# FFN up projections as a 2x2 block product in seven products

## Chip, core and metric

The program runs on one core of one Trainium2 chip. The metric is device time in microseconds (us): the median over repeated executions.

## What is computed

One inference step of a two-layer decoder trunk for 512 prompt tokens and 8 x 4 sample tokens, all 544 handled together. Each layer has a gated FFN, a mixing stage (two head-wise recurrences and an LRU branch, then an output projection) and a second gated FFN:

```python
def _swiglu(xn, w_in, w_out):
    gu = xn @ w_in                        # 1024 -> 2 * 2816
    g, u = gu[..., :D_FF], gu[..., D_FF:]
    return (jax.nn.silu(g) * u) @ w_out   # 2816 -> 1024

x = x + 0.5 * _swiglu(_rmsnorm(x, norm_ffn1), w_ffn1_in, w_ffn1_out)
x = x + merged @ w_out                    # the mixing stage
x = x + 0.5 * _swiglu(_rmsnorm(x, norm_ffn2), w_ffn2_in, w_ffn2_out)
```

So an execution has four FFNs: FFN1 and FFN2 of each of two layers. All data are float32.

## The kernel before

Activations lie transposed: `x` is 128 partitions x 8 k tiles x 544 tokens. A float32 product is made of three TensorE passes over operands split into a high part and a low part (the rest): high by high, low weight by high x, high weight by low x (`three_pass`, its matmuls are L415). The names are `wh`, `wl` for the parts of a weight block and `xh`, `xl` for those of x. TensorE takes 272 tokens per matmul, so each k tile costs three passes times two token halves.

An FFN has 22 up blocks. An up block has 2048 columns of weights (8 k tiles, each with 128 columns for g and 128 for u), and gives two output tiles: g into the PSUM pair `stream_a`, u into `stream_b`, 48 matmuls each. The 22 blocks go in two halves, 12 and 10 (`FF_HALVES`). After each half, eight down tiles (one for each k tile of x) multiply the hidden tiles `hh`, `hl` of that half by the down weights and are added to x.

Weights go through two slots. SyncE loads a block into `stage` (L328) as soon as the slot's low part has been made; ScalarE makes the high part (`split_hi`, L847) as soon as TensorE has left the slot's last block; VectorE makes the low part (`split_lo`, L1156) and so releases TensorE for that block. Between these, in program order on each engine:

- VectorE, per up block: g times the root-mean-square factor `rstd` (L1147, `gs`), u times `rstd` (L1147, `us`), their product with the SiLU (L1203), its high part (L1205) and low part (L1206), then the low part of the weights of two blocks on.
- ScalarE, per up block: SiLU (L904), then the high part of a weight block.
- VectorE, per down tile: x plus half the tile (`residual`, L1176). In the second half of an FFN and in the output projection, ScalarE then makes the high part of the new x with the norm's weight (L851) and its square (L892), VectorE the low part (L1162) and the running sum of squares `acc` (L1171). After the last one TensorE sums `acc` over the partitions (L448), ScalarE takes the root, VectorE its reciprocal (L1187).

The wait that orders TensorE behind the weights is `block_ready`; the wait that orders it behind an emptied PSUM pair is on `tile_free`. Register, semaphore and branch instructions stand in the loops (`Fori`); the last block or tile of a loop is written out behind it.

Of the kernel before, what the change touches and what calls it, by code (L numbers as in the profile page):

```python
# [51 lines left out]
FF_HALVES = [12, 10]  # L52
assert sum(FF_HALVES) * P == FF
W_SLOT = 2048


FFN_BLOCKS = sum(FF_HALVES) + 2 * KT
FFN_TILES = 2 * sum(FF_HALVES) + 2 * KT
# [22 lines left out]
STORES = 2 + HEADS * 3 + HEADS * 2 + 4  # L81

# [8 lines left out]
class Chain:  # L91
# [22 lines left out]
    def link(self, ins):  # L114
        self.n += 1
        ins.then_inc(self.sem, 1)
        self.eng.wait_ge(self.sem, self.n)
# [5 lines left out]
def trunk(nc, x_T, w_up1, w_down1, w_mix, w_gates, w_o, w_up2, w_down2, vec, b_if, w_lr2, w_ra, w_ri, consts, level_masks,  # L123
          m0, c0, n0, s0, h0, conv0, o_y, o_pc, o_pm, o_ps, o_ph, o_pconv,
          o_sc, o_sn, o_sm, o_ss, o_sh, o_sconv, rows_dram):
    with ExitStack() as ctx:
# [8 lines left out]
        xh = sb("xh", [P, KT, N], F32R)  # L135
        xl = sb("xl", [P, KT, N], F32R)
        stage = sb("stage", [P, 2, W_SLOT])
        wh = sb("wh", [P, 2, W_SLOT], F32R)
        wl = sb("wl", [P, 2, W_SLOT], F32R)
# [7 lines left out]
        sq = sb("sq", [P, N])  # L147
        xg = sb("xg", [P, N])
# [27 lines left out]
        hh = sb("hh", [P, FF_HALVES[0], N], F32R, ff)  # L176
        hl = sb("hl", [P, FF_HALVES[0], N], F32R, ff)

        gwh, gwl = (t[:, FF_HALVES[1]:FF_HALVES[0], :].rearrange("p t n -> p (t n)")[:, 0:GATE_W] for t in (hh, hl))
        gs = sb("gs", [P, N], where=ff)  # L180
        us = sb("us", [P, N], where=ff)
        sg = sb("sg", [P, N], where=ff)
        hp = sb("hp", [P, N], where=ff)
        gstage = sb("gstage", [P, GATE_W], where=ff)
        ff.close()

# [28 lines left out]
        mh = sb("mh", [P, KT, N], F32R, lru)  # L215
        ml = sb("ml", [P, KT, N], F32R, lru)
# [11 lines left out]
        scv = sb("scv", [P, KT, SEQS, 3], where=lru)  # L228
        lru.close()
# [5 lines left out]
        pair = [psum("stream_a", [P, 2, 512]), psum("stream_b", [P, 2, 512])]  # L235
        Q = psum("mix", [P, 4, 512])

# [12 lines left out]
        first_low = sem("first_low_parts")  # L250
# [53 lines left out]
        first_sq = [merged[:, m, :] for m in range(KT)]  # L304
# [8 lines left out]
        def banks(p):  # L313
            return p[:, :, 0:HALF]

# [6 lines left out]
        def _(sp):  # L322
# [7 lines left out]
            def ffn(L, first, w_up, w_down, gates=False):  # L330
                n = L * LAYER_BLOCKS + first
                up = down = 0
                for half, tiles in enumerate(FF_HALVES):
                    if gates and half == 1:
                        sp.dma_start(gstage[:], w_gates[L]).then_inc(gate_loaded, 16)
# [8 lines left out]
                    n = n + tiles  # L344
                    up += tiles
                    with sp.Fori(0, KT // 2) as i:
                        for j in range(2):
                            load(i * 2 + (n + j), j, w_down[L, i * 2 + (down + j), :, 0:tiles * P])
                    n = n + KT
                    down += KT  # L350

            sp.wait_ge(init_done, 1)
            for L in range(DEPTH):
                ffn(L, 0, w_up1, w_down1, gates=True)
# [6 lines left out]
                ffn(L, BLK_FFN2, w_up2, w_down2)  # L361
# [10 lines left out]
        def _(pool):  # L372
# [5 lines left out]
            pool.memset(ones[:], 1.0)  # L378
            pool.memset(one_t[:], 1.0).then_inc(split_done, 2)
# [30 lines left out]
        def _(pe):  # L410
# [10 lines left out]
            def tile(t, slot, k_tiles, width, col, act=(xh, xl), weights=(wh, wl), late=None, fresh=None,  # L421
                     count=1, ks=None, low=None):
# [5 lines left out]
                if ks[0] == 0:  # L428
                    pe.wait_ge(tile_free, t + 1)
                for k in ks:  # L430
                    if late and k >= k_tiles - 2:
                        late(k_tiles - 1 - k)
                    if low is not None:
                        pe.wait_ge(low, k + 1)
# [10 lines left out]
            def norm_squares():  # L445

                for h in range(2):
                    mm = pe.matmul(Q[:, h, 0:HALF], ones[:], acc[:, h * HALF:(h + 1) * HALF], start=True, stop=True)  # L448
                return mm

            def first_block(n, t, j, norm):

                parts = (wh[:, j], wl[:, j])
                block_ready(n)
                tile(t, 0, KT, 2 * P, 0, weights=parts, low=first_low)
                tile(t + 1, 1, KT, 2 * P, P, weights=parts, ks=range(KT // 2))
                pe.wait_ge(acc_ready, norm)
                norm_squares().then_inc(norm_sum, 1)
                tile(t + 1, 1, KT, 2 * P, P, weights=parts, ks=range(KT // 2, KT))

            def ffn_in_block(L, n, t, j, norm=None):
                if norm == KT:
                    return first_block(n, t, j, norm)
                block_ready(n)
                tile(t, 0, KT, 2 * P, 0, weights=(wh[:, j], wl[:, j]), fresh=norm)
                if norm is not None:
                    pe.wait_ge(acc_ready, norm)
                    norm_squares().then_inc(norm_sum, 1)
                tile(t + 1, 1, KT, 2 * P, P, weights=(wh[:, j], wl[:, j]))

            def ffn(L, first, first_tile, h_base, norm):
                n = L * LAYER_BLOCKS + first
                t = L * LAYER_TILES + first_tile
                hd = L * (2 * sum(FF_HALVES)) + h_base
                for half, tiles in enumerate(FF_HALVES):
                    start = 0
                    if half == 0:
                        for j in range(2):
                            ffn_in_block(L, n + j, t + 2 * j, j, norm if j == 0 else None)
                        start = 1  # L480
                    with pe.Fori(start, tiles // 2) as i:
                        for j in range(2):
                            ffn_in_block(L, i * 2 + (n + j), i * 4 + (t + 2 * j), j)
# [1425 lines left out]
```

## Time and profile before

| | |
|---|---|
| median of 3 runs | 3124.23 us (3123.17 to 3125.16) |
| profiled execution: span from the first to the last instruction | 3122.4 us |
| what lies around that span, by the median | 1.8 us |
| TensorE matmul busy | 3063.6 us, 98% |
| VectorE busy | 1902.3 us, 61% |
| ScalarE busy | 1039.4 us, 33% |
| granted TensorE clock, mean | 0.995 |

The profile's busy time of TensorE counts pipelined matmuls, so the pace of a stage is read from the times at which its tiles end. The profiled execution has no time of its own on record beside the span; the difference to the median stands in the table. PE is TensorE, PEld its weight load, DVE is VectorE, ACT is ScalarE, SP is SyncE.

### The profile page before, as it was taken

How to read it: one execution, taken by the hardware profiler on the slowest of the kernel's cores; microseconds unless marked ns; L12 is line 12 of the kernel's file. 1: busy time of each engine (PE TensorE's matmuls, PEld its weight loads, DVE VectorE, ACT ScalarE, POOL GpSimd, SP SyncE). 2: the span in 40 equal slices, each digit the busy share in tenths (PEclk: the TensorE clock that was granted, in tenths of full speed). 3: DMA queues.
4: the chain of work that ended last, by engine and by line, in shares of the span. 5: the costliest groups of instructions: out<-in, count | busy, mean ns of one | idle time of the engine just before them, and what ended most of it. 6: DMA issues, size and time to landing. Idle time of an engine off the chain costs nothing.

```text
span 3122.4 us, 60368 instructions
## 1 busy us (share of the span) xinstructions
PE 3063.6 (98%) x25824; PEld 3014.0 (97%) x25824; DVE 1902.3 (61%) x2705; ACT 1039.4 (33%) x992; POOL 12.9 (0%) x36
## 2 busy tenths in 40 slices
PE   7999999999999999999999999999999999999998
PEld 7999999999999999999999999999999999999997
DVE  5434467778788874434454344677878788643344
ACT  3222232334334652212232122333334466321212
POOL 1000000000000000000000000000000000000000
PEclk9999999999999999999999999999999999999999
DMA  3222233233222222222222222233222222222222
GB/s 141 78 95 94 72 112 109 107 110 111 97 86 91 86 83 95 78 98 76 86 95 81 101 89 73 105 111 134 92 98 98 85 97 80 95 81 84 91 79 71
DMA packets 51915, 292.18 MB, mean 94 GB/s; under 512 B 9384, under 2 KB 12264, under 8 KB 23880
## 3 DMA queue, kind: packets, MB, share of 16 engines
q1 hardware_dynamic: 37152, 241.43, 22.4%
q10 hardware_dynamic: 13984, 48.48, 4.1%
q8 instruction: 90, 1.47, 0.2%
q0 software_dynamic: 656, 0.52, 0.1%
q14 instruction: 33, 0.27, 0.0%
HBM read 268.90 MB, written 21.50 MB: 93 GB/s over the span
## 4 chain that ended last, share of the span: by engine, by line
PE 88%; DVE 7%; ACT 2%; issue 1%; DMA 1%; DVEq 0%; ACTq 0%; POOL 0%; POOLq 0%
PE stream_b L415 38%; PE stream_a L415 38%; PE stream_a L502 4%; PE mix L787 1%; DVE wl L1156 1%; PE stream_b L508 1%; PE mix L623 1%; PE mix L563 1%; PE mix L707 1%; PE mix L544 1%; PE mix L626 1%; PE mix L556 0%; DVE rstd L1187 0%; PE mix L734 0%; DMA seven<-rows_scratch 0%
## 5 line engine op out<-in xcount | busy, mean ns | idle before, releaser
L847 ACT ACTIVATE wh<-stage 128x2048 fp32r<-128x2048 f32 (+2 forms) x246 | 435.9, 1772 | 800.0 <-PE stream_b L415 588.1
L1156 DVE TENSOR_TENSOR wl<-stage,wh 128x2048 fp32r<-128x2048 f32 (+2 forms) x248 | 525.8, 2120 | 93.6 <-ACT wh L847 69.2
L415 PE MATMUL stream_a<-xh,wh 128*128 128x272 f32 x2560 | 536.2, 291 | 18.6 <-DVE xl L1162 13.1
L415 PE MATMUL stream_b<-xh,wh 128*128 128x272 f32 x2560 | 541.2, 293 | 0.0
L415 PE MATMUL stream_a<-xl,wh 128*128 128x272 f32 x2560 | 531.1, 289 | 0.0
L415 PE MATMUL stream_b<-xl,wh 128*128 128x272 f32 x2560 | 530.0, 288 | 0.0
L415 PE MATMUL stream_a<-xh,wl 128*128 128x272 f32 x2560 | 529.5, 288 | 0.0
L415 PE MATMUL stream_b<-xh,wl 128*128 128x272 f32 x2560 | 528.3, 288 | 0.0
L415 PEld LDWEIGHTS stream_a<-xh,wh 128*128 128x128 f32 x2560 | 404.2, 189 | 22.4 <-DVE wl L1156 13.1
L415 PEld LDWEIGHTS stream_b<-xh,wh 128*128 128x128 f32 x2560 | 403.6, 188 | 7.3 <-issue 3.3
L415 PEld LDWEIGHTS stream_a<-xh,wl 128*128 128x128 f32 x2560 | 403.7, 189 | 0.0
L415 PEld LDWEIGHTS stream_b<-xh,wl 128*128 128x128 f32 x2560 | 402.7, 189 | 0.0
L415 PEld LDWEIGHTS stream_a<-xl,wh 128*128 128x128 f32 x2560 | 401.4, 189 | 0.0
L415 PEld LDWEIGHTS stream_b<-xl,wh 128*128 128x128 f32 x2560 | 400.2, 189 | 0.0
L1147 DVE TENSOR_TENSOR us<-stream_b,rstd 128x544 f32<-128x544 f32 x88 | 63.8, 725 | 446.4 <-PE stream_b L415 446.1
L904 ACT ACTIVATE sg<-gs 128x544 f32<-128x544 f32 x88 | 58.0, 660 | 401.1 <-DVE gs L1147 401.1
L415 PE MATMUL stream_a<-hh,wh 128*128 128x272 f32 x704 | 146.0, 289 | 0.0
L415 PE MATMUL stream_b<-hh,wh 128*128 128x272 f32 x704 | 146.0, 289 | 0.0
L415 PE MATMUL stream_a<-hh,wl 128*128 128x272 f32 x704 | 145.6, 288 | 0.0
L415 PE MATMUL stream_b<-hh,wl 128*128 128x272 f32 x704 | 145.6, 288 | 0.0
L502 PE MATMUL stream_a<-wh,xl 128*128 128x256 f32 x512 | 144.7, 283 | 0.0
L415 PE MATMUL stream_a<-hl,wh 128*128 128x272 f32 x704 | 144.1, 286 | 0.0
(349 smaller groups left out, 4367.6 us busy)
## 6 DMA issues: line engine op xcount, KB each, us to landing
stage<-in_w_mix SPq DMA_DIRECT2D x88, 1024.0 KB, 4.8
stage<-in_w_up SPq DMA_DIRECT2D x87, 1024.0 KB, 4.8
stage<-in_w_down SPq DMA_DIRECT2D x32, 768.0 KB, 4.2
stage<-in_w_down SPq DMA_DIRECT2D x32, 640.0 KB, 3.9
CS<-in_c ACTq DMA_DIRECT2D x8, 1024.0 KB, 4.7
out_o_sc<-CS ACTq DMA_DIRECT2D x8, 1024.0 KB
CS<-in_s ACTq DMA_DIRECT2D x8, 1024.0 KB, 4.8
out_o_ss<-CS ACTq DMA_DIRECT2D x8, 1024.0 KB
```

The source lines that it names most:

```text
L415: mm = [pe.matmul(out(h), a(h), b(h), start=f, stop=z) for h in range(2)]
L502: mm = pe.matmul(out, a[:, k, tok], b[:, j, k * DV:(k + 1) * DV], start=f, stop=z)
L508: mm = pe.matmul(pair[1][:, 0, 0:DV], both[:, k * 2 * NS:k * 2 * NS + P], b[:, j, k * DV:(k + 1) * DV], start=f, stop=z)
L544: mm = pe.matmul(Q[g * NS:(g + 1) * NS, b_, 0:DV], Qm[:, s_ * NS:(s_ + 1) * NS], CS[:, s_, :], start=s_ < 4, stop=s_ >= 4)
L563: mm = pe.matmul(Q[:, b_ + h, 0:HALF], ones[:], src[:, h * HALF:(h + 1) * HALF], start=True, stop=True)
L623: mm = pe.matmul(Q[:, v, sl], here, wS[:, sl], start=True, stop=c == 0)
L626: mm = pe.matmul(Q[:, v, sl], before, qs[:, sl], start=False, stop=True)
L707: mm = pe.matmul(Q[g * G:(g + 1) * G, 1 + r // 4, o:o + G], lhs[:, k0:k0 + G], rhs[:, k0:k0 + G], start=True, stop=True)
L847: act.activation(wh[:, slot, 0:width], stage[:, slot, 0:width], ACT.Copy).then_inc(hi_done, 1)
L904: act.activation(sg[:], gs[:], ACT.Silu).then_inc(silu_done, 1)
L1147: ins = tt_(halves(dst), banks(pair[slot]), rs2, ALU.mult)
L1156: tt_(wl[:, slot, 0:width], stage[:, slot, 0:width], wh[:, slot, 0:width].bitcast(F32), ALU.subtract).then_inc(split_done, 1)
```

## The change

In an up block the k tiles are taken in pairs (even, odd) and the tokens in halves. That makes g and u of 128 columns a 2x2 by 2x2 block product, and seven products in place of eight give it. Each product is four k-tile pairs times three passes on 272 tokens, 12 matmuls, so a block has 84 matmuls in place of 96. The products need sums and differences of blocks:

- of the weights: four sums `S` per block (VectorE, L1399, L1405, L1406), whose high part ScalarE and whose low part VectorE makes (L955, L1422); three blocks are used as they are (`wx_high`, `wx_low`, L946, L1418). `S` lies in the same memory as `wl`.
- of x: four sums `XT` per pair of k tiles, with high and low parts (`x_side`), made once per FFN where x is updated ahead of it.
- of the products: ScalarE copies the first product into the third bank (`seed`) and keeps the second in `p5s` (`keep_fifth`); VectorE adds `p5s` to the running third bank twice (`sum_fifth`, L1413), into bank 1 and bank 3, on which the fifth to seventh products then go on. TensorE waits for each of these inside the block.

Blocks use the four banks of `stream` and the four of `mix` in turn. The hidden product is left without the second `rstd`, which `residual_scaled` now puts on the down tile (L1488), with the addition to x in an instruction of its own (L1491). The high part of the hidden tile moves to ScalarE; its low part stays on VectorE. The 22 blocks go in four parts (4, 6, 6, 6) with eight down tiles after each.

```diff
-FF_HALVES = [12, 10]
+FF_PARTS = [4, 6, 6, 6]
...
+        S = sb("w_sums", [P, 2, W_SLOT], F32, own)
+        own.close()
         wl = sb("wl", [P, 2, W_SLOT], F32R)
...
         # TensorE
+            def product(B, bank, w, q, x, seeded, base=None, step=0):
+                for kt in range(PAIRS):
...
+                    for a, b, f, z in ((0, 0, True, False), (1, 0, False, False), (0, 1, False, True)):
+                        mm = pe.matmul(B[:, bank, 0:HALF], w[a][:, kt, q, :], x[b][:, kt, :],
+                                       start=f and kt == 0 and not seeded, stop=z and kt == PAIRS - 1,
+                                       skip_group_check=True)
...
+                block_ready(n)
+                pe.wait_ge(tile_free, t + freed)
+                product(B, 0, pure, 2, xp[0], False, base, 1).then_inc(prod_done, 1)
+                product(B, 1, sums, 0, xt[0], False, base, 2).then_inc(prod_done, 1)
...
+                pe.wait_ge(copied, 2 * u + 1)
+                product(B, 2, sums, 2, xt[1], True, base, 3).then_inc(prod_done, 1)
+                product(B, 0, pure, 0, xp[1], True, base, 4).then_inc(prod_done, 1)
+                pe.wait_ge(seeded, 2 * u + 1)
+                product(B, 2, sums, 1, xt[2], True, base, 3).then_inc(prod_done, 1)
+                product(B, 1, sums, 3, xp[2], True, base, 4).then_inc(prod_done, 1)
+                pe.wait_ge(seeded, 2 * u + 2)
+                product(B, 2, pure, 1, xt[3], True, base, 5).then_inc(tile_done, 2)
...
         # ScalarE, per up block
+                            gate(tj)
+                            pure_high(i + (nh + 1), j, tj + 1, 0)
+                            pure_high(i + (nh + 1), j, tj + 1, 1)
+                            seed(uj + 1, 1 - j, tj + 2, 0)
+                            hidden_high(tj, uj, i * 2 + j)
+                            keep_fifth(uj + 1, 1 - j)
+                            sums_high(uj + 2, j, 0)
+                            sums_high(uj + 2, j, 1)
...
         # VectorE
+            def into_up(nh, u, j):
+                begun = weight_sums(nh, j)
+                more_sums(j, begun)
+                up_low(2 * nh + j, u, j, (lambda: sum_fifth(u - 1, 0, 1)) if j else None)
+                if j:
+                    sum_fifth(u - 1, 0, 3)
...
+            def up_block(t, u, a, j, nh, plain):
+                B = sets[j]
+                dve.wait_ge(prod_done, (PRODUCTS - 1) * u + 6)
+                tt_(halves(gs[:]), banks(B[:, 0:2]), rs2, ALU.mult).then_inc(tile_free, 1)
+                if not plain:
+                    begun = weight_sums(nh, j)
+                dve.wait_ge(silu_done, u + 1)
+                tile_ready(t + 1)
...
+                tt_(halves(hp[:]), halves(sg[:]), banks(B[:, 2:4]), ALU.mult).then_inc(tile_free, 1)
...
+                else:
+                    more_sums(j, begun)
+                    up_low(nh * 2 + j, u + 2, j, lambda: sum_fifth(u + 1, 1 - j, 1))
+                    hidden_low(u, a)
+                    sum_fifth(u + 1, 1 - j, 3)
```

How this stands on VectorE, at three places. First the loop over up blocks: `gs` is now called `xg`, and each row is one instruction with the semaphores that it waits for. Before, one block (written-out end of a half):

```order
L1147 TENSOR_TENSOR gs<-stream_a,rstd 128x544 [waits tile_done]
L1147 TENSOR_TENSOR us<-stream_b,rstd 128x544 [waits tile_done,tile_free]
L1203 TENSOR_TENSOR hp<-sg,us 128x544 [waits silu_done,tile_free]
L1205 CAST hh<-hp 128x544 [waits dve_chain]
L1206 TENSOR_TENSOR hl<-hp,hh 128x544 [waits dve_chain]
L1156 TENSOR_TENSOR wl<-stage,wh 128x1536 [waits hi_done,h_done]
```

and of the change, one block whose slot is filled with another up block:

```order
L1526 TENSOR_TENSOR xg<-stream,rstd 128x544 [waits product_done]
L1399 TENSOR_TENSOR w_sums<-stage 128x4x256 [waits block_loaded_0]
L1533 TENSOR_TENSOR hp<-sg,stream 128x544 [waits h_done,product_seeded,tile_done,silu_done]
L1405 TENSOR_TENSOR w_sums<-stage,w_sums 128x4x128 [waits dve_chain]
L1406 TENSOR_TENSOR w_sums<-stage,w_sums 128x4x128 [waits dve_chain]
L1418 TENSOR_TENSOR wx_low<-stage,wx_high 128x1536 [waits pure_high]
L1413 TENSOR_TENSOR mix<-mix,p5s 128x272 [waits product_copied,product_done]
L1422 TENSOR_TENSOR wl<-w_sums,wh 128x2048 [waits hi_done]
L1520 TENSOR_TENSOR hl<-hp,hh 128x544 [waits hh_done]
L1413 TENSOR_TENSOR mix<-mix,p5s 128x272 [waits product_copied,product_done]
```

The four weight sums, two low parts in place of one and the two additions of `p5s` for the block that TensorE works on have come in between; the multiplication of u and the high part of the hidden tile have gone.

Second the end of a run of down tiles, where the slot of the seventh down tile is filled with the first up block of the next part. Before:

```order
L104 REGISTER_ALU
L111 ISA
L1176 SCALAR_TENSOR_TENSOR x<-stream_a,x 128x544 [waits tile_done]
L1156 TENSOR_TENSOR wl<-stage,wh 128x2048 [waits hi_done,tile_free]
L1176 SCALAR_TENSOR_TENSOR x<-stream_b,x 128x544 [waits tile_done]
L1156 TENSOR_TENSOR wl<-stage,wh 128x2048 [waits hi_done,tile_free]
```

and now, of the first of these two slots and the beginning of the second:

```order
L1488 SCALAR_TENSOR_TENSOR sg<-stream,rstd 128x544 [waits tile_done]
L1491 TENSOR_TENSOR x<-x,sg 128x544 [waits tile_free]
L1399 TENSOR_TENSOR w_sums<-stage 128x4x256 [waits block_loaded_0,x_updated]
L1405 TENSOR_TENSOR w_sums<-stage,w_sums 128x4x128 [waits dve_chain]
L1406 TENSOR_TENSOR w_sums<-stage,w_sums 128x4x128 [waits dve_chain]
L1418 TENSOR_TENSOR wx_low<-stage,wx_high 128x1536 [waits pure_high]
L1422 TENSOR_TENSOR wl<-w_sums,wh 128x2048 [waits hi_done]
L1488 SCALAR_TENSOR_TENSOR sg<-stream,rstd 128x544 [waits tile_done]
L1491 TENSOR_TENSOR x<-x,sg 128x544 [waits tile_free]
```

Two instructions between the end of a down tile and the release of the slot have become seven.

Third the output projection ahead of FFN2. There a block of weights gives two tiles, and after each tile x is updated and prepared for the next stage. Before, the second tile of the loop's last block:

```order
L1176 SCALAR_TENSOR_TENSOR x<-stream_b,x 128x544
L1161 REGISTER_ALU [waits tile_free]
L1162 ISA [waits xh_ready]
L1162 SCALAR_TENSOR_TENSOR xl<-x,vectors,xh 128x544
L1171 TENSOR_TENSOR acc<-acc,sq 128x544 [waits sq_ready]
L1155 REGISTER_ALU [waits acc_ready]
L1156 TENSOR_TENSOR wl<-stage,wh 128x2048 [waits hi_done]
```

and now, the second tile of a block and the slot's next up block:

```order
L1496 SCALAR_TENSOR_TENSOR x<-stream,x 128x544 [waits tile_done]
L1446 TENSOR_TENSOR xt<-x_scaled 128x272 [waits xh_ready,tile_free]
L1447 TENSOR_TENSOR xt<-xt,x_scaled 128x272 [waits dve_chain]
L1451 TENSOR_TENSOR xt<-x_scaled,xt 128x272 [waits x_sums]
L1471 TENSOR_TENSOR acc<-acc,sq 128x544 [waits sq_ready]
L1460 TENSOR_TENSOR xt_low<-xt,xt_high 128x544 [waits x_high,x_sums,acc_ready]
L1462 TENSOR_TENSOR xp_low<-x_scaled,xp_high 128x544 [waits x_high]
L1466 TENSOR_TENSOR xt_low<-xt,xt_high 128x272 [waits x_high]
L1399 TENSOR_TENSOR w_sums<-stage 128x4x256 [waits block_loaded_0]
L1405 TENSOR_TENSOR w_sums<-stage,w_sums 128x4x128 [waits dve_chain]
L1406 TENSOR_TENSOR w_sums<-stage,w_sums 128x4x128 [waits dve_chain]
L1418 TENSOR_TENSOR wx_low<-stage,wx_high 128x1536 [waits pure_high]
```

After each first tile of a pair VectorE has one sum and two low parts, after each second one three sums and three low parts, before the weights of the slot; the second slot's `wl` is followed by the reciprocal (L1507) as before.

## Rows read from the trace of the kernel before

**Rows 1.** Page, busy time by engine and chain that ended last
```profile
PE 3063.6 (98%) x25824; PEld 3014.0 (97%) x25824; DVE 1902.3 (61%) x2705; ACT 1039.4 (33%) x992; POOL 12.9 (0%) x36
PE 88%; DVE 7%; ACT 2%; issue 1%; DMA 1%; DVEq 0%; ACTq 0%; POOL 0%; POOLq 0%
```

**Rows 2.** Chain in order of time: start us, us, what
```profile
31.14 0.14 issue
31.27 7.78 PE stream_a L415 x48
...
57.09 6.01 PE stream_a L415 x48
...
505.15 11.40 PE stream_a L502 x96
...
1310.83 9.00 PE stream_a L415 x72
```

**Rows 3.** Chain in order of time, FFN2 of layer 0 into FFN1 of layer 1
```profile
1555.60 7.50 PE stream_b L415 x60
1563.10 6.01 PE stream_a L415 x48
1569.12 0.92 PE mix L448 x4
```

**Rows 4.** VectorE groups by line and shape: count, busy us, mean ns, idle before
```profile
L1156 DVE TENSOR_TENSOR wl<-stage,wh 128x2048 fp32r<-128x2048 f32 x184 | 421.8, 2292 | 71.5 <-ACT wh L847 49.3 <-ACT wh L857 8.5
L1156 DVE TENSOR_TENSOR wl<-stage,wh 128x1536 fp32r<-128x1536 f32 x32 | 56.3, 1758 | 16.0 <-ACT wh L847 15.6
L1343 DVE TENSOR_TENSOR Kws<-K,seqm 128x1024 fp32r<-128x1024 f32 x16 | 19.5, 1221 | 0.3
L1206 DVE TENSOR_TENSOR hl<-hp,hh 128x544 f32 x72 | 52.3, 726 | 8.8
L1444 DVE TENSOR_TENSOR Kw<-mix,seven 128x512 f32<-128x512 f32 x8 | 5.5, 692 | 0.3
L1624 DVE TENSOR_TENSOR lxp<-stream_b,rstd 128x272 f32<-128x272 f32 x8 | 3.5, 440 | 0.2
L1187 DVE RECIPROCAL rstd<-sd 128x544 f32<-128x544 f32 x6 | 21.3, 3554 | 7.2 <-ACT sd L882 5.4 <-DVE Qm L1739 1.8
```

**Rows 5.** ScalarE groups by line and shape, same columns
```profile
L916 ACT ACTIVATE hh<-gstage 128x1024 fp32r<-128x1024 f32 x2 | 2.1, 1044 | 0.0
L892 ACT ACTIVATE sq<-x 128x544 f32 x40 | 25.8, 645 | 35.5 <-DVE x L1176 35.5
L851 ACT ACTIVATE xh<-x,vectors x34 | 25.5, 750 | 162.7 <-DVE x L1176 162.7
L979 ACT ACTIVATE hsq<-mix 128x256 f32<-128x256 f32 x8 | 3.1, 384 | 39.4 <-PE mix L544 39.4
```

**Rows 6.** Timeline of VectorE: start us, us, instruction, idle before
```profile
12.21 2.87 DVE L1162 SCALAR_TENSOR_TENSOR xl<-x,vectors,xh 128x544 fp32r<-128x544 f32 x4
...
59.44 0.73 DVE L1206 TENSOR_TENSOR hl<-hp,hh 128x544 f32 x1
60.28 2.29 DVE L1156 TENSOR_TENSOR wl<-stage,wh 128x2048 fp32r<-128x2048 f32 x1
```

**Rows 7.** Windows, TensorE: stretch, us, busy (count), granted clock, DMA share, GB/s
```profile
27.00:31.00 4.00, 1.51 (x13) 1.00 0.64 247
33.00:34.00 1.00, 1.00 (x7) 0.50 0.00 0
```

**Rows 8.** DMA issues: count, KB each, median us to landing
```profile
stage<-in_w_down SPq DMA_DIRECT2D x32, 640.0 KB, 3.9
wra<-in_w_ra ACTq DMA_DIRECT2D x4, 256.0 KB, 2.7
```

**Rows 9.** Timeline of ScalarE at the start: start us, us, instruction
```profile
7.98 1.91 ACT L857 ACTIVATE wh<-stage 128x2048 fp32r<-128x2048 f32 x1
9.79 2.65 ACT L851 ACTIVATE xh<-x,vectors 128x544 fp32r<-128x544 f32 x4
```

More of the change, by code:

```diff
@@ L328, in load, with ffn @@
                 sp.dma_start(stage[:, slot, 0:width], src).then_inc(block_loaded[slot], 16)
-            def ffn(L, first, w_up, w_down, gates=False):
+            def ffn(L, first, first_tile, w_up, w_down, gates=False, swapped=False):
                 n = L * LAYER_BLOCKS + first
[L332 to L335, printed above, removed]
+                t = L * LAYER_TILES + first_tile
+                up = 0
+                for part, tiles in enumerate(FF_PARTS):
                     begun = 0
@@ L925, in ffn @@
-                    with act.Fori(0, KT // 2 - 1) as i:
-                        down(i, tiles * P)
-                    down(KT // 2 - 1, 0 if last and half == 1 else 2 * D)
-                    t, nh = t + KT, nh + KT // 2
+                    i = KT // 2 - 1
+                    for j in range(2):
+                        arrived(i, j)
+                        if end and next_ffn is None:
+                            if not last:
+                                plain_high(i + (nh + 1), j, i * 2 + (t + j), 2 * D)
+                        else:
+                            into_up(i + (nh + 1), j, i * 2 + (t + j), u + j, t + KT,
+                                    norm + 1 if end else None)
@@ L1191, in ffn, with up @@
+            def ffn(L, first, first_tile, u, norm, g_col, gates=False, next_ffn=None, last=False):
+                nh = L * (LAYER_BLOCKS // 2) + first // 2
                 t = L * LAYER_TILES + first_tile
[L1192 removed]
                 reciprocal_norm(norm)
[L1194 to L1196 removed]
+                for part, tiles in enumerate(FF_PARTS):
+                    def up(i, plain=0):
                         chain.restart()
@@ L1214, in ffn, with down @@
+                    if part == 0 and gates and L == 0:
                         decay_rates()
-                    n, t, hd = n + tiles, t + 2 * tiles, hd + tiles
-                    if gates and half == 1:
+                    t, nh, u = t + 2 * tiles, nh + tiles // 2, u + tiles
+                    end = part == len(FF_PARTS) - 1
+                    if end:
+                        clear_acc()
+                    def down(i, ahead):
+                        chain.restart()
+                        for j in range(2):
+                            swapped = end and next_ffn is not None
+                            m = i * 2 + (1 - j if swapped else j)
+                            n_sq = norm * KT + i * 2 + (KT + j)
+                            residual_scaled(i * 2 + (t + j), j, m, i * 2 + (down_tiles(L, first) + part * KT + j + 1))
+                            if swapped:
+                                x_side(i, j, n_sq, next_ffn)
+                            elif end:
+                                prepare(m, g_col + m, n_sq, not last)
+                            ahead(i, j)
@@ new lines, in plain, with next_stage @@
+                    def plain(i, j):
+                        split_lo(i * 2 + (2 * nh + 2 + j), j, tiles * P)
+                    def next_stage(i, j):
+                        if not end or next_ffn is not None:
+                            into_up(i + (nh + 1), u + j, j)
+                        elif not last:
+                            split_lo(i * 2 + (2 * nh + 2 + j), j, 2 * D)
+                    with dve.Fori(0, KT // 2 - 1) as i:
+                        down(i, plain)
+                    if gates and end:
```

538 lines of the change are left out of this document (383 added, 155 removed).

## Prediction

> **What bounds the kernel now.** I read the page first: TensorE is busy 98% of the span, VectorE 61%, ScalarE 33%, and the chain that ended last lies 88% on TensorE [rows 1]. Then the chain in order of time: an up tile of 48 matmuls takes 6.01 us, a down tile of 72 takes 9.00 [rows 2], so 0.125 us a matmul of 272 columns wherever nothing is waited for. The hand-over from one FFN to the next shows no gap: 1555.60 + 7.50 is 1563.10, and 1563.10 + 6.01 is 1569.12 within rounding [rows 3]. Removed matmuls are therefore worth their full time, as long as VectorE and ScalarE keep up. They do so easily now: a block lasts 12.02 us and VectorE needs about 5.6 of it (three instructions of 0.725, one copy, one low part of 2.29 [rows 4]). So the prediction is made on VectorE's lists.
>
> **What is removed.** 88 up blocks lose 12 matmuls each: 1056 x 0.1253 = **-132.3 us**. The runs of 12 into one bank cost no more: a tile whose matmuls go 24 in a row into one bank has 96 of 256 columns in 11.40 us [rows 2], 0.1188 each, which is the 272-column pace less 16 columns at 2.4 GHz.
>
> **Prices.** Two-operand VectorE work costs 2.29 us for 2048 columns, 1.76 for 1536, 1.22 for 1024, 0.73 for 544, 0.69 for 512, 0.44 for 272 [rows 4]; 768 lies at 0.96, 1088 at 1.29, 2176 at 2.42 on the same line. ScalarE: 1.04 for 1024, 0.65 for a square of 544, 0.75 for a scaled copy of 544, 0.38 for 256 out of PSUM [rows 5], so 0.41 for 272. A gap between two VectorE instructions is 0.12 where loop registers are set on a wait, and -0.07 where four independent ones overlap (4 x 0.785 took 2.87) [rows 6]; I take 0 inside a list and 0.04 where engines hand over. VectorE writing to PSUM has no row: 0.44 as for reading it, at least the same line's fixed part of 0.16, at most twice 0.44.
>
> **Inside an up part.** An up block is 7 products of 1.503, 10.52 us. VectorE's ten instructions make 9.7 us. What closes the loop is one chain: seventh product of a block, first and second of the next (4.51), ScalarE keeps the second product (0.41) and only then, in its order, makes the high parts of the sums (2 x 1.04), VectorE the low part (2.29), the hidden low part (0.73), and the second addition (0.44), for which the next seventh product waits. With hand-overs that is 10.7, so 0.2 a block. Twelve such blocks an FFN, beside those in the starts below: 48 x 0.2 = **+10**. (Gaps of -0.07: 0; of 0.12: 0.8 each, 38.)
>
> **Twelve boundaries from down tiles to up blocks.** The sums for the next part lie in the memory of the low weights that the seventh down tile reads, and stand behind that tile's eviction on VectorE. From its end: eviction 0.73, addition 0.73, sums 1.22 + 0.69 + 0.69, ScalarE's high parts 2.09, low part 2.29, and six hand-overs: 8.7 us until the block may start. TensorE has only the eighth down tile to cover it: 36 matmuls, 4.5 us, after a part of six; 24, 3.0 us, after the part of four. Before, the same wait was one high and one low part under a tile of 7.5 or 9.0 us. So 8 x 4.2 + 4 x 5.7 = 56, and the first block then waits 0.24 for its first addition, since VectorE comes to it 6.25 us after the start and four products take 6.01: **+59**. (Bounds 53 to 77, by the gaps.)
>
> **Output projection into FFN2, twice.** Per first tile of a pair VectorE has 0.73 (x), a wait for ScalarE's square and scaled copy (1.40), 0.44, 0.72 and two of 0.44: 4.2 us; per second tile 0.73, 1.40, three of 0.44, 0.72, two of 0.73, 0.44: 6.1; two tiles and a low part of weights come to about 13 against 12 us of TensorE, which delays the projection by 1.4. From the start of its last block VectorE still has both tiles of the third (10.3), the sums and low parts of the first slot (7.0 with ScalarE), both tiles of the fourth (10.3), then 4.4 and the addition 0.44 before the fifth product: 33.7 with hand-overs, against 12.0 + 0.92 + 6.01 on TensorE. That is 14.8. Behind it the reciprocal (3.55) stands ahead of the next round, so the second block's first addition comes 9.8 us after the first block's last addition, 2.3 after the products that should cover it; 0.5 more in the third. **+38** in all. (30 to 54.)
>
> **FFN2 of layer 0 into FFN1 of layer 1.** The same preparation now hangs on down tiles of 4.5 us: 5.9 and 7.8 us a pair with eviction, addition and a weight part of 0.96, some 14 with hand-overs against 9.0, for three pairs: 15. Then as above from the eighth tile: 4.9 + 7.0 + 6.8 + 4.4 + 0.44 and hand-overs, 24, against 11.4, and 3 for the reciprocal: 16. **+31.** (27 to 42.)
>
> **FFN1 into the mixing stage, twice.** Eviction, addition, high part, low part, sum and weights make 5.0 against 4.5 a tile: 2, and 2.5 until the gates' tile has the last squares: **+9**. (7 to 16.)
>
> **Start.** ScalarE can begin at 7.98 and scales four k tiles in 2.65 [rows 9]; with 1.49, 2.09 and twice 2.65 all of x is scaled at 16.9. From there VectorE has seven of 1.29, two of 2.42, seven of 0.72 and two additions, 20 us plus waits: 38; then the second slot's 7.0: the second block begins at 45. Its first addition stands behind reciprocal and round, 55; it ends at 60, the third at 71. Before, the third block ended at 57.09 [rows 2]. 14, and 4.5 that the first term already counts: **+18**. (14 to 24.) The last eviction adds an instruction: +1.
>
> **The clock.** At 31.27 a tile took 7.78 in place of 6.01 [rows 2], after a stretch in which TensorE worked 1.51 of 4 us; the clock granted was 1.00 before and 0.50 within the tile [rows 7]. That wait was shorter than any of the twelve. So I charge each boundary 1.77 less the 0.24 it hides: **+18** (0 to 21). The Trainium skill says likewise (TensorE: Matmul & The Clock Gate, "HAM oscillation — how this bites in real kernels") that matmul bursts with waits between pay the slow clock burst by burst. The trace agrees at that one tile; read strictly, it applies to the waits inside the four FFN starts too, and the sum would be 3194 in place of 3176.
>
> **Hidden.** The down weights: a slot's load is issued after the low part, 2.4 us behind a tile's end, and has two tiles less that time; 256 KB landed in 2.7 and 640 KB in 3.9 [rows 8], against 3.6 in the part of four and 6.6 in those of six. ScalarE's new high part of the hidden tile takes 0.65 of a 10.7 us round in which it works 5.9. If the loads weren't covered, up to 1 us for each of 24 tiles.
>
> **Sum.** -132.3 + 10 + 59 + 38 + 31 + 9 + 18 + 1 + 18 = +52 on the profiled 3122.4: 3174; with the 1.8 that the median lies above the span, **3176 us**, slower by 1.7%. A difference of 0.2%, 6 us, is about what can be told from none.
>
> **Rivals.**
> - *VectorE's instructions overlap throughout* and the clock stays up: all terms at their lower ends, 0 + 53 + 30 + 27 + 7 + 14 + 1 = 132, which is just the gain: 3124. For it: four independent ones did overlap [rows 6]; against it: most of the new ones wait for another engine or for their predecessor. 0.08.
> - *Faster: the x sums hide.* If VectorE and ScalarE prepare x and the sums under the tiles they follow, as they do now at hand-overs without a gap [rows 3], the terms of projection, FFN change, mixing and start (96) fall away: 3080. It decides as soon as less than half of them is left. Against it: the lists are two to three times the tiles. 0.10.
> - *Every wait inside a block restarts TensorE.* Four waits a block; the tile at 31.27 began 0.14 after its releaser [rows 2], and if each cost that, 88 x 4 x 0.14 = 49 more: 3225. Against it: a tile that found both its waits fulfilled took 6.01 [rows 2]. 0.10.
> - *The clock rule in the starts*: ten more such stretches, two or three a start, of 1.77 each: 3194. For it, the tile at 31.27; against it, TensorE waits for VectorE's list there whatever its clock. 0.15.
> - *The sum as it stands*, give or take the gaps: 0.57.
>
> **Chances and range.** Faster 0.12 (the second rival and a tail of the first), same 0.04, slower 0.84. Range 3130 to 3235: it leaves out the first two rivals below, and above it gaps of 0.12 everywhere (38 + 77 + 54 + 42 + 16 + 24 + 1 + 21 = 273, so 3265).
>
> **What would show it.** In the profile after: 24,768 matmuls and a few; seven-product blocks of 10.5 to 10.8 us; a TensorE wait of 4 to 6 us on `wl` at each of twelve boundaries; waits of TensorE that sum to over 10 us on x parts and additions at each of the four FFN starts (kernel start, two projections, FFN2 into FFN1); half clock behind the boundaries; VectorE busy near all of the FFNs. I am wrong if blocks last over 11 us (the loop's chain), if the boundaries show no wait (the sums begin earlier than I read), or if the starts cost under 10 us each.

## The result, and the profile after

The changed kernel takes 3184.89 us in the median (3184.57 to 3189.59, 4 runs), the kernel before 3123.7 on the same chip: a ratio of 1.0199, with a 95% interval of 1.0185 to 1.0214. It is slower by 61 us. The profiled execution spans 3182.9 us, 60.5 more than before.

The page of the changed kernel, busy time by engine and the chain that ended last, which answers to [rows 1]:

```profile
PE 2996.2 (94%) x24772; PEld 2934.1 (92%) x24772; DVE 2409.8 (76%) x3398; ACT 1316.6 (41%) x1629; POOL 13.3 (0%) x37
...
PE 76%; DVE 14%; ACT 6%; issue 3%; DMA 1%; DVEq 0%; ACTq 0%; POOL 0%; POOLq 0%
```

There are 1052 matmuls fewer, but the chain now lies 20% on VectorE and ScalarE, against 9% before. What TensorE waits for, longest sums first (us in all, times, longest):

```profile
PE stream L518 <- DVE wl L1422: 70.1, 15, 5.7
PE stream L474 <- DVE wl L1378: 26.3, 18, 6.7
PE stream L518 <- DVE xp_low L1437: 17.1, 3, 16.0
PE stream L474 <- DVE sg L1488: 8.1, 2, 4.0
PE mix L518 <- ACT mix L963: 7.0, 4, 1.9
```

The first line is the low part of the weight sums: twelve boundaries between parts (55.7 us) and three of the FFN starts (14.4). One boundary after a part of six, as the chain of the changed kernel in order of time (start us, us, what); the waits here have no counterpart in [rows 3]:

```profile
218.31 0.74 DVE sg L1488
...
219.06 0.74 DVE x L1491
...
219.82 1.24 DVE w_sums L1399
...
221.08 0.70 DVE w_sums L1405
...
221.81 0.70 DVE w_sums L1406
...
223.50 1.05 ACT wh L955
...
224.57 2.30 DVE wl L1422
226.87 0.04 issue
226.92 13.07 PE stream L518 x84
...
282.21 10.55 PE mix L518 x84
```

The seventh down tile ends at 218.28 and the eighth at 222.78; the block starts at 226.92. In between, 8.6 us, stands the list of the prediction, link by link. The first block then takes 13.07 us, the later ones 10.55. The windows of the same stretch (us, busy of PE, PEld, DVE, ACT, POOL, then the granted clock, the DMA share and GB/s), beside [rows 7]:

```profile
222.00:227.00 5.00, 0.86 (x8) 0.64 (x6) 4.60 (x4) 2.52 (x3) 0.00 (x0) 0.82 0.00 0
227.00:232.00 5.00, 5.00 (x22) 5.00 (x23) 4.42 (x6) 1.34 (x2) 0.00 (x0) 0.50 0.58 210
232.00:240.00 8.00, 8.00 (x66) 8.00 (x65) 5.77 (x6) 2.95 (x4) 0.00 (x0) 1.00 0.20 63
```

For five microseconds behind the wait the granted clock is 0.50, which is 1.2 GHz: 22 matmuls where a full clock gives 40.

The terms of the sum against what the two traces show:

| step of the prediction | predicted, us | measured, us | worked out from |
|---|---|---|---|
| removed matmuls | -132 | -132 | 1056 at the pace of [rows 2] |
| rounds inside a part | +10 | +2 | 10.55 a block against 84 x 0.1253 = 10.52, some 72 blocks |
| twelve boundaries | +59 | +56 | waits of 4.14 after eight parts of six and 5.64 after four of four |
| the clock | +18 | +29 | twelve first blocks, 12.4 to 13.5 each, together 155.9, against 12 x 10.55 |
| projection into FFN2, twice | +38 | +29 | last wait of mixing to end of the fourth block: 96.8 and 98.1 against 89.2 and 88.9, plus 6.0 removed from each |
| FFN2 into FFN1 | +31 | +31 | 109.7 from the last block of FFN2 to the fourth of FFN1, against 36.1 + 0.9 + 42.1 |
| FFN1 into mixing, twice | +9 | +18 | last up block to the sum of squares: 52.2 and 52.5 against 67.3 before, less the 24.1 of down matmuls that now lie in earlier parts |
| start | +18 | +19 | fourth block ends at 81.9 against 69.1, plus 6.0 removed |
| end | +1 | 0 | 53.6 from the last up block to the end against 77.2, less 24.0 of down matmuls that now lie in earlier parts |
| not in the sum: constants of the gates | 0 | +9 | first eight down tiles 33.1, those of the other parts of four 24.5 |
| sum | +52 | +61 | span: +60.5 |

The forecast's +59 for the boundaries holds 12 x 0.24 for the first addition, which lies in the first block and so in the measured 29: the waits alone were forecast at 56 and took 56.

### The profile page after: what moved, and what is told of

It is laid out like the page before. It is cut to its first block, busy times and chain, and to the rows that moved or that the text cites. A ratio compares the mean times of both kernels' runs of the same rounds, so it can differ in the third digit from the quotient of the medians.

```text
span 3182.9 us, 61006 instructions
## 1 busy us (share of the span) xinstructions
PE 2996.2 (94%) x24772; PEld 2934.1 (92%) x24772; DVE 2409.8 (76%) x3398; ACT 1316.6 (41%) x1629; POOL 13.3 (0%) x37
## 4 chain that ended last, share of the span: by engine, by line
PE 76%; DVE 14%; ACT 6%; issue 3%; DMA 1%; DVEq 0%; ACTq 0%; POOL 0%; POOLq 0%
PE stream L474 35%; PE stream L518 14%; PE mix L518 14%; PE stream L585 4%; DVE wl L1378 1%; DVE wl L1422 1%; ACT wh L955 1%; DVE sg L1488 1%; PE mix L870 1%; DVE x L1491 1%; PE stream L591 1%; PE mix L706 1%; PE mix L646 1%; ACT wh L934 1%; DVE rstd L1507 1%
## 5 line engine op out<-in xcount | busy, mean ns | idle before, releaser
L474 PE MATMUL stream<-xh,wh 128*128 128x272 f32 x2304 | 492.1, 295 | 2.5 <-DVE val L1681 2.5
L474 PE MATMUL stream<-xl,wh 128*128 128x272 f32 x2304 | 476.8, 288 | 0.0
L474 PE MATMUL stream<-xh,wl 128*128 128x272 f32 x2304 | 475.7, 288 | 0.6 <-issue 0.6
L474 PEld LDWEIGHTS stream<-xh,wh 128*128 128x128 f32 x2304 | 362.9, 188 | 12.9 <-issue 6.9
L1378 DVE TENSOR_TENSOR wl<-stage,wh 128x768 fp32r<-128x768 f32 (+2 forms) x224 | 334.0, 1491 | 48.2 <-ACT wh L934 32.3
L474 PEld LDWEIGHTS stream<-xh,wl 128*128 128x128 f32 x2304 | 361.9, 188 | 0.8 <-issue 0.8
L474 PEld LDWEIGHTS stream<-xl,wh 128*128 128x128 f32 x2304 | 360.2, 189 | 0.0
L474 PE MATMUL stream<-hh,wh 128*128 128x272 f32 x1408 | 295.8, 291 | 26.6 <-DVE wl L1378 26.3
L474 PE MATMUL stream<-hl,wh 128*128 128x272 f32 x1408 | 292.8, 290 | 0.0
L474 PE MATMUL stream<-hh,wl 128*128 128x272 f32 x1408 | 292.4, 289 | 0.0
L1422 DVE TENSOR_TENSOR wl<-w_sums,wh 128x2048 fp32r<-128x2048 f32 x88 | 201.7, 2292 | 28.9 <-ACT wh L955 28.3
L955 ACT ACTIVATE wh<-w_sums 128x1024 fp32r<-128x1024 f32 x176 | 175.9, 1049 | 37.3 <-DVE w_sums L1406 37.3
L1488 DVE SCALAR_TENSOR_TENSOR sg<-stream,rstd 128x544 f32<-128x544 f32 x128 | 92.5, 723 | 122.9 <-PE stream L474 122.5
```

What stands on the lines that cost most here:

```text
L474: mm = [pe.matmul(out(h), a(h), b(h), start=f, stop=z) for h in range(2)]
L955: ins = act.activation(quads(wh, slot, a, b), quads(S, slot, a, b), ACT.Copy)
L1378: tt_(wl[:, slot, 0:width], stage[:, slot, 0:width], wh[:, slot, 0:width].bitcast(F32), ALU.subtract).then_inc(split_done, 1)
L1422: tt_(wl[:, slot, :], S[:, slot, :], wh[:, slot, :].bitcast(F32), ALU.subtract).then_inc(split_done, 1)
L1488: ins = stt(halves(sg[:]), banks(pair[slot]), 0.5, rs2, ALU.mult, ALU.mult)
```

## The experiments

All are timed against the kernel before on the same chip, which took 3122.9 to 3124.1 us beside them; differences are to the 3184.9 of the changed kernel, unless said otherwise.

**The parts alone** (e1_parts). The kernel before, cut into the parts of the changed one; eight products, none of the sums.

```diff
-FF_HALVES = [12, 10]
+FF_HALVES = [4, 6, 6, 6]
```

> The kernel before with parts of 4, 6, 6, 6 in place of 12, 10 and nothing else: eight products, no sums. Theory A (the boundary stall is the list sums, high parts, low part that stands behind the eviction): from a seventh down tile's end only eviction 0.73, ScalarE's high part 2.0 beside it and the low part 2.29 remain, 4.4 us against 4.5 of cover after a part of six and 3.0 after the part of four; so about 0 at eight boundaries, 1.4 and a slow-clock 1.8 at four, the constants of the gates 7 to 9 once, 2 to 6 at hand-overs: 3124 + 15 to 28, 3139 to 3152. Rival B (short parts cost this by themselves): most of the 85 us that the boundaries of the changed kernel show, 3190 to 3210.

Measured: 3159.4 us, ratio 1.0118 (1.0101 to 1.0135), 36.5 more than before. Its chain at the boundary that was shown above:

```profile
206.29 4.50 PE stream_b L417 x36
210.79 0.04 issue
210.84 4.27 PE stream_a L417 x32
```

No wait after a part of six (0.04 us), 2.0 to 2.1 after a part of four. So rival B falls: short parts don't make the stall, the sums do. Theory A was too low by 8 us at its upper end; some of that lies at the two hand-overs into mixing, where TensorE waits 2.6 us for an eviction (1.0 before). Of the 193 us that the changed kernel pays for its 132, about 36 are the parts' and 157, the rest, come with the seven products.

**TensorE kept at work during the wait** (e2_warm). Extra matmuls on x parts into a bank that nothing reads then, ahead of the first block of a part: 42 behind the part of four, 30 behind those of six.

```diff
+                for _ in range(warm):
+                    pe.matmul(Q[:, 3, 0:HALF], XTH[:, 0, 0, 0:P], XTH[:, 0, 0, :], start=True, stop=True)
                 B = sets[j]
...
-                                 stage_no if first_of_all else None, norm if first_of_all else None)
+                                 stage_no if first_of_all else None, norm if first_of_all else None,
+                                 0 if part == 0 or j else 42 if part == 1 else 30)
```

> The changed kernel, with 30 (after a part of six) or 42 (after the part of four) extra matmuls of 272 columns into an unused bank while TensorE waits at each of the twelve boundaries; 3.8 and 5.3 us of the waits of 4.1 and 5.6. Theory A (the clock falls because TensorE stands still there): the first block of a part goes from 13.0 back to 10.6 to 10.8 us, 12 x 2.3 = 27 less: 3156 to 3160. Rival B (the clock falls there for another reason, such as the burst of loads that begins just then): blocks stay at 12.5 to 13, 3180 to 3185.

Measured: 3162.9, ratio 1.0129 (1.0112 to 1.0146), 22 less. The same boundary, windows and chain:

```profile
219.00:223.00 4.00, 4.00 (x34) 3.97 (x32) 3.59 (x3) 2.53 (x3) 0.00 (x0) 1.00 0.00 0
223.50:234.00 10.50, 10.46 (x82) 10.39 (x83) 9.63 (x11) 3.99 (x6) 0.00 (x0) 1.00 0.34 109
```

```profile
223.50 0.04 issue
223.54 10.94 PE stream L518 x84
234.48 10.55 PE mix L518 x84
```

The clock granted stays at 1.00 and the first block takes 10.94 in place of 13.07, all twelve alike (together 131.2 in place of 155.9); the burst of loads (DMA share 0.34 over this block) is still there, so it wasn't that. Theory A, with 0.4 us a block left over at full clock; the forecast had 0.24 of it, for the first addition.

**The sums ahead of the eviction** (e3_early). For the first block of the second to fourth part the sums go to memory of their own, and VectorE makes them and the low part of the three blocks that are used as they are (the pure part) before it waits for the seventh down tile; in the down tiles of these parts the addition to x follows the weights.

```diff
+                            if not end and ahead is plain:
+                                residual_scaled(i * 2 + (t + j), j, m, updated, lambda: plain(i, j))
+                                continue
+                            if not end and j == 0:
+                                slot_no = i + (nh + 1)
+                                more_sums(0, weight_sums(slot_no, 0, first_quads), first_quads)
...
+                                residual_scaled(i * 2 + (t + j), j, m, updated, first_low)
+                                continue
```

> The changed kernel; the weight sums of the first block of the second to fourth part lie in memory of their own and are made before the seventh down tile ends, with the pure parts; behind its eviction only ScalarE's two high parts and the low part remain, and the additions to x stand behind the weights. Theory A (the list behind the eviction is the stall): after a part of six the wait falls from 4.1 to 0 to 0.9, and with it the slow clock, 8 x (3.7 + 2.4) = 49 less; after the part of four the load comes too late, 0 to 1 less each: 3131 to 3140. Rival B (the block's load, 4.8 us, lands only at the tile's end, so that the sums can't be earlier): waits of 3 to 4 stay, 3175 to 3183.

Measured: 3148.8, ratio 1.0080 (1.0063 to 1.0097), 36 less. VectorE at the boundary:

```profile
214.60 1.23 DVE L1411 TENSOR_TENSOR first_sums<-stage 128x1024 f32<-128x1024 f32 x1 [0.37 <-DVE x L1506]
...
217.20 1.75 DVE L1598 TENSOR_TENSOR wx_low<-stage,wx_high 128x1536 fp32r<-128x1536 f32 x1
218.86 0.72 DVE L1501 SCALAR_TENSOR_TENSOR sg<-stream,rstd 128x544 f32<-128x544 f32 x1
219.61 2.29 DVE L1602 TENSOR_TENSOR wl<-first_sums,wh 128x2048 fp32r<-128x2048 f32 x1
```

The wait after a part of six falls from 4.14 to 1.2 us (the eighth down tile ends at 220.74, the low part at 221.9) and the first block runs at full clock though the loads are under way (window, columns as above):

```profile
222.00:227.00 5.00, 5.00 (x40) 5.00 (x41) 4.83 (x7) 1.94 (x4) 0.00 (x0) 1.00 0.62 213
```

From the end of the down tiles to the end of the part it saves 4.3 us, eight times. After a part of four it saves 0.3 to 1.5, near the 0 to 1 that was expected because the load lands too late. Theory A, but 9 us beyond its range: 1.2 is over its 0 to 0.9, and the first block's first addition, which stands in VectorE's list among the weights of the second block, now comes 0.6 late.

**The scaled copy ahead of the square** (e4_swap). Where x is prepared for seven products, on ScalarE; shown for the second tile of a pair, the first has the same.

```diff
-                act.activation(sq[:], x[:, m, :], ACT.Square).then_inc(sq_ready, 1)
                 if second:
                     scaled(XG[:, 1:3, :], m, g_col)
+                    act.activation(sq[:], x[:, m, :], ACT.Square).then_inc(sq_ready, 1)
```

> The changed kernel; where x is prepared for seven products (two projections, FFN2 into FFN1) ScalarE makes the scaled copy before the square, so VectorE's x sums wait 0.65 us less in each of 8 tiles. Theory A (VectorE's list of x parts sets these starts): 4 to 8 tiles x 0.65 = 2.6 to 5.2 a start, three starts, 8 to 15 less: 3170 to 3177. Rival B (the weights' loads or ScalarE set them): 0 to 3 less, 3182 to 3185.

Measured: 3173.8, ratio 1.0164 (1.0147 to 1.0181), 11 less. VectorE's first x sum of a second tile, in the changed kernel and then here:

```profile
1184.28 0.44 DVE L1446 TENSOR_TENSOR xt<-x_scaled 128x272 f32<-128x272 f32 x1 [1.44 <-ACT x_scaled L972]
```

```profile
1180.50 0.44 DVE L1447 TENSOR_TENSOR xt<-x_scaled 128x272 f32<-128x272 f32 x1 [0.89 <-ACT x_scaled L972]
```

Some 0.55 us less idle time at each of 24 tiles makes 13 us, and TensorE gets 11 of it. Theory A: VectorE's list sets these starts.

**The down weights ahead of x** (e5_plainfirst). Behind an FFN's last part, on VectorE as shown and with the high parts on ScalarE likewise.

```diff
+                            if ahead is plain:
+                                plain(i, j)
                             if swapped:
                                 x_side(i, j, n_sq, next_ffn)
...
-                            ahead(i, j)
+                            if ahead is not plain:
+                                ahead(i, j)
```

> The changed kernel; behind an FFN's last part the weights of the next down tile are split right after the addition to x (ScalarE's high part ahead of its work on x), so that VectorE's low part of 0.96 lies in the time in which it now waits for ScalarE's square and scaled copy. Theory A (these hand-overs are VectorE's list with ScalarE's copies in it): FFN1 into mixing falls from 5.0 to 4.1 us a tile, under the 4.5 of TensorE, so 9 goes to 2 to 4, twice; FFN2 into FFN1 loses 0.96 to 1.3 in each of six tiles, 6 to 9: 16 to 23 less, 3162 to 3169. Rival B (TensorE's 4.5 us tiles or the loads of the down weights set them): 0 to 4 less.

Measured: 3171.4, ratio 1.0153 (1.0137 to 1.0168), 13.5 less, between the theories. TensorE's waits from FFN2 into FFN1, in the changed kernel and then here:

```profile
PE stream L474 <- DVE wl L1378: 14.0, 5, 3.9
PE stream L518 <- DVE wl L1422: 5.3, 1, 5.3
```

```profile
PE stream L518 <- DVE wl L1422: 11.6, 1, 11.6
PE stream L474 <- DVE wl L1378: 4.1, 3, 1.9
```

The down tiles wait 10 us less, and the first up block 6.3 more; the hand-over, measured as in the table, takes 105.5 us in place of 109.7. FFN1 into mixing takes 48.8 and 48.4 in place of 52.2 and 52.5. The list is what binds, but its end decides: of a shorter wait in the middle most is given back there.

**The constants of the gates** (e6_consts). Behind the second part, with one exponential and one logarithm for both layers.

```diff
-                    if part == 0 and gates and L == 0:
+                    if part == 1 and gates and L == 0:
```

> The changed kernel; the constants of the gates (once, layer 0) are made behind the second part in place of the first, with two table loads in place of four. Theory A (the 6.7 us wait of the third down tile of the first part is ScalarE's constants, which down tiles of 3.0 us don't cover): 8 to 9 less, 3176. Rival B (that wait is the down weights' load or the start's backlog): no change, 3182 to 3186.

Measured: 3177.7 (3173.1 to 3181.4), ratio 1.0167 (1.0152 to 1.0183), 7 less. ScalarE behind the first part of the changed kernel:

```profile
84.01 1.28 ACT L927 ACT_TABLE_LOAD   x1
85.30 0.21 ACT L927 ACTIVATE c<-c 128x8 f32<-128x8 f32 x1
85.53 1.28 ACT L928 ACT_TABLE_LOAD   x1
...
90.26 1.13 ACT L934 ACTIVATE wh<-stage 128x512 fp32r<-128x512 f32 x2
```

Four table loads of 1.28 us hold the weights of the third down tile until 90.3. Without them the eight down tiles take 24.5 us in place of 33.1, and the second part's lose 1.9 of that: 6.7 less. The profiled run took 3181.2 us, near the upper end of the range: it gives 2.8 us back from FFN2 into FFN1 (112.5 in place of 109.7), at a granted clock of 0.89 against 0.94 over 111 us. Theory A. The Trainium skill (ScalarE: Activation LUTs, "Table sets: the hidden batching unit") says to batch calls by table set. The trace agrees: with one exponential and one logarithm two loads stand there, at 179.82 and 181.41 us, in place of four, 1.28 us each.

**One more VectorE instruction in the loop** (e8_slack). 0.64 us, to see how near the loop's chain is to binding.

```diff
                     up_low(nh * 2 + j, u + 2, j, lambda: sum_fifth(u + 1, 1 - j, 1))
+                    tt_(sd[:], hp[:], hp[:], ALU.subtract)
                     hidden_low(u, a)
```

> The changed kernel with one more VectorE instruction of 544 columns (0.64 after the last one) in each round whose slot takes another up block (14 an FFN, 56 in all), between the low part of the sums and the low part of the hidden tile; it writes to memory that nothing reads there. Theory A (one chain closes the loop, as predicted, but with some 0.4 us to spare: the second addition ends 0.38 ahead of the seventh product): 56 x 0.25 = 14 more, 3199. Rival B (the predicted chain of 10.7, nothing to spare): 56 x 0.64 = 36 more, 3221. Rival C (only VectorE's total counts, 9.9 of 10.55): no change, 3185.

Measured: 3220.8, ratio 1.0311 (1.0295 to 1.0326), 36 more: rival B's figure, and my theory A fell. One block in the windows of the changed kernel, and one here:

```profile
345.96:356.51 10.55, 10.55 (x86) 10.55 (x86) 9.19 (x11) 5.48 (x8) 0.00 (x0) 1.00 0.28 99
```

```profile
360.07:371.21 11.14, 10.82 (x85) 10.61 (x85) 9.82 (x12) 5.41 (x8) 0.00 (x0) 1.00 0.26 93
```

A block grows by 0.59 us; 56 of them make 33 of the 36, and the other 3 weren't traced. VectorE works 9.8 of 11.1 us, so its total isn't the bound (rival C). The 0.38 us to spare I had taken from the end of a block less twelve matmuls. That was read wrongly, since the wait stands on the weight load. The end of the list on VectorE in the changed kernel, and the weight load that waits for its last addition:

```profile
351.33 2.29 DVE L1422 TENSOR_TENSOR wl<-w_sums,wh 128x2048 fp32r<-128x2048 f32 x1 [0.28 <-ACT wh L955]
353.54 0.72 DVE L1520 TENSOR_TENSOR hl<-hp,hh 128x544 f32 x1
354.18 0.45 DVE L1413 TENSOR_TENSOR mix<-mix,p5s 128x272 f32<-128x272 f32 x1
...
354.72 0.19 PEld L518 LDWEIGHTS mix<-xt_high,wx_high 128*128 128x128 f32 x1
```

The addition ends at 354.63. 0.09 us, less a hand-over, is all that the loop has to spare. Once TensorE does wait, as in e8_slack, the weight load and its matmul start together, and the next matmul comes 0.23 us later in place of 0.125:

```profile
360.07 0.19 PEld L518 LDWEIGHTS mix<-xt_high,wx_high 128*128 128x128 f32 x1 [0.53 <-DVE mix L1413]
360.07 0.39 PE L518 MATMUL mix<-xt_high,wx_high 128*128 128x272 f32 x1 [0.31 <-DVE mix L1413]
360.30 0.29 PE L518 MATMUL mix<-xt_high,wx_low 128*128 128x272 f32 x1
```

**All edits together** (e7_all): the early sums, the swap, the down weights first, the constants, and 36 extra matmuls at the boundaries behind a part of four.

> The changed kernel with the early sums, the scaled copy ahead of the square, the down weights ahead of x, the constants moved, and 36 extra matmuls at the four boundaries behind a part of four. If the terms add (36 + 11 + 12 to 18, the second and third sharing some 4, + 8 + 8): 3104 to 3112, faster than the kernel before by 0.4 to 0.6%. If they overlap (each removes the same waits): 3125 to 3135.

Measured: 3112.4, ratio 0.9963 (0.9950 to 0.9977). 72.5 less: the four edits measured alone make 36.1 + 11.1 + 13.5 + 7.2 = 68, and the extra matmuls behind the parts of four, which weren't measured alone, were put at 8; there the first block takes 11.7 us against 12.6 to 13.3 in e3_early. So the terms add to within 4 us, the part that the second and the third were expected to share, and the case in which they remove the same waits (3125 to 3135) falls. Two more edits (e9_best):

```diff
                 more_sums(j, begun)
+                if mid and j:
+                    sum_fifth(u - 1, 0, 1)
+                up_low(2 * nh + j, u, j, (lambda: sum_fifth(u - 1, 0, 1)) if j and not mid else None)
...
+                        if ahead is not plain and to_mix:
+                            for j in range(2):
+                                ahead(i, j)
```

> The kernel of all five edits, and two more: in a part's second block the first addition stands ahead of the pure low part, and at FFN1 into mixing the two low parts of 2048 columns stand behind the last down tile's x parts instead of ahead of its eviction. If each of the waits left is VectorE's order: 12 x 0.6 and 2 x 3.7 less, 3098 to 3100. If other waits take their place: 3108 to 3114.

Measured: 3101.2 (3099.9 to 3102.3), ratio 0.9926 (0.9912 to 0.9939): faster than the kernel before by 0.7%, and 1 us above what was expected if VectorE's order sets these waits. TensorE's waits that are left, longest first:

```profile
PE stream L524 <- DVE xp_low L1456: 16.7, 2, 16.1
PE stream L524 <- DVE wl L1441: 16.0, 3, 9.5
PE stream L524 <- DVE wl L1612: 11.1, 12, 1.2
PE stream L524 <- DVE stream L1432: 8.3, 15, 1.8
```

The first is the wait for the weights and x at the start, which the kernel before has as well (13.1 us); the second is FFN2 into FFN1 and the projections; the third is the boundaries, 1.2 us each behind the parts of six and 0.3 behind the extra matmuls. The waits for the additions (last line) fell from 11.5 us (e7_all) to 8.3, less than the 7 expected: where the first addition of a first block was 0.6 late, the second one is now 0.3 late. The hand-over into mixing gave more, since its slow clock went with its wait (1.7 in place of 4.8 us, and the tile behind it 6.2 in place of 8.6).

## Why the prediction was right

3176 was forecast with a range of 3130 to 3235, and 3184.9 came. The direction, the places and the mechanism are those of the text; some sizes aren't, and they offset one another: terms that were 21 us too high in all stand against 30 too low. That the sum came within 9 us, in a range of 105, is luck to that extent.

- *Removed matmuls, full pace.* Right: blocks of 84 matmuls take 10.55 us, and runs of twelve into one bank cost nothing.
- *Inside an up part.* The chain that closes the loop was named rightly; in e8_slack 0.59 of an added 0.64 us is paid. It was sized 10.7 and is about 10.5, because VectorE's instructions that wait for nothing overlap: the low part of the hidden tile and the second addition each start 0.08 us before the instruction ahead of them ends. I had taken 0 inside a list though [rows 6] show an overlap for independent ones; I had worked out -0.07 from four instructions, but they have three gaps, which makes -0.09. 8 us too high. (Of a block before I counted three instructions of 0.725; there are four, and the 5.6 us hold with four.)
- *Twelve boundaries.* 56 of 59, and of 56 without the first addition. e3_early takes most of it away behind the parts of six by moving the sums, e1_parts shows none of it without them after a part of six.
- *The clock.* Right in cause: e2_warm takes 25 of the 29 us away. 11 us too low, 8 with the first addition set against it: the half clock lasts 5 us here, and I had priced it by the 1.77 us of one tile of before. The Trainium skill (TensorE: Matmul & The Clock Gate, "HAM oscillation — how this bites in real kernels") has bursts of matmuls with waits between pay the slow clock burst by burst. The trace agrees at each of the twelve. Behind the eight waits of 1.2 us in e3_early the clock stays at 1.00.
- *Projection into FFN2.* 9 us too high. From the start of the projection's last block VectorE's list took 30.5 us, not 33.7: two tiles of a pair take 9.8, not 10.3, by the same overlaps. e4_swap shows that it is this list.
- *FFN2 into FFN1, start, end.* As predicted, within 1 us. But TensorE had the half clock in the FFN starts too (granted 0.50 to 0.52 for 7 us from 27.0, 7 from 44.25, 13.5 from 1194.5, 3.5 from 1604.0 and 6.5 from 1614.5), for which these terms hold nothing; no run separates what it cost there from the waits, so part of this agreement may be chance.
- *FFN1 into mixing.* 9 us too low. The backlog of 5.0 against 4.5 a tile was right, but I left out that the eviction of the last down tile stands on VectorE behind a low part of 2048 columns for mixing, so the gates' tile waits 4.0 us (1.0 before) and then runs at the slow clock for another 1.5. e9_best takes most of this away by order alone. That tile before and now:

```profile
418.63 6.24 PE stream_b L415 x48
```

```profile
443.10 7.78 PE stream L474 x48
```

- *The constants of the gates.* Missed: 9 us. They stood behind the first part before, too, under two down tiles of 9.0 us; with tiles of 3.0 that cover is gone. I had asked that question of the down weights' loads, not of everything that ScalarE does there.

The rivals: the overlap of VectorE's instructions is real but worth some 0.08 us at a time, so the lower ends of all terms didn't come together; the x sums don't hide; a wait inside a block doesn't occur at all in the steady loop, so its restart cost nothing. The clock rule in the starts (3194) has the half clock on its side, but projection, FFN change and start came to 79 us against 87 without any charge for it; that its cost hides behind VectorE's list, as was argued, is not shown, and the 2.8 us in e6_consts speak against hiding all of it.

## What to carry to other kernels

Before fewer matmuls are bought with sums on another engine, write down that engine's list at every place where the pipeline drains and refills (starts, part boundaries, hand-overs), not only in the loop: here the loop cost 2 us and those places 191. A list behind an eviction is shortened by order first: what needs only loaded data goes ahead of the wait, and what nobody waits for goes behind the release. When tiles become shorter, ask again for every piece of work that used to lie under the longer ones.

## What was not expected of the hardware

- The half clock behind a wait of 4.1 us lasted 5 us (2.5 us lost, 0.4 of which stay in e2_warm at full clock), longer than the 3.5 or so behind the one of before (1.77 lost); 30 matmuls of no use in the wait kept the clock at 1.00 and saved 22 us in the whole kernel.
- A wait inside a block costs more than its length: in e8_slack the first matmul behind it takes 0.23 us in place of 0.125; its weight load, which otherwise starts 0.12 ahead of it (354.72 against 354.84 in the changed kernel), starts only with it.
- VectorE's two-operand addition of SBUF to a PSUM bank, which had no row before, takes 0.44 to 0.45 us for 272 columns, as the read of PSUM does in [rows 4].
